# One input projection's start rearranged: w_in stored in order of use on 256-byte rows, x's first tile and the first weights on two queues, and four of k's eight contraction tiles as f16 halves

## What is computed

```python
def first_block(x, pre_mix_norm, w_in, ...):
    xn = _rms_norm(h, pre_mix_norm[l])          # over the 1024 features of a token
    proj = (xn @ w_in[l]).astype(jnp.float32)   # 1024 x 3336
    p_ssd, p_rwkv = jnp.split(proj, [SSD_COLS], axis=-1)
    y_ssd = _ssd_mixer(p_ssd, ...)
    y_rwkv = _rwkv7_mixer(p_rwkv, ...)
    ...
```

## Time and profile before

| | us |
|---|---|
| median of 3 executions | 740.94 |
| lowest, highest | 739.91, 741.89 |
| the profiled execution | 741.43 |
| its span, first to last instruction | 739.6 |
| PE busy in the span | 730.2 (99%) |
| DVE, ACT, POOL busy | 563.0, 434.7, 47.2 |
| bytes moved | 129.43 MB, mean 175 GB/s |

### The profile page before, as it was taken

One profiled execution on the slowest core, in us unless ns is written; L12 is line 12 of the kernel. 1 busy time (PEld: TensorE's weight loads), 2 busy tenths in 40 slices (PEclk: granted clock), 3 DMA queues, 4 the chain that ended last, 5 costly groups with the idle time before them and its releaser, 6 DMA issues.

```text
span 739.6 us, 16490 instructions
## 1 busy us (share of the span) xinstructions
PE 730.2 (99%) x7072; PEld 597.5 (81%) x7072; DVE 563.0 (76%) x893; ACT 434.7 (59%) x690; POOL 47.2 (6%) x81
## 2 busy tenths in 40 slices
PE   9999999999999999999999999999999999999997
PEld 7888877889778888888877696898888888865553
DVE  5699976777879999997668797889685666762453
ACT  5599872523667676666556573387483755653342
POOL 0000133040020000000002000003003000000000
PEclk9999999999999999999999999999999999999999
DMA  9990303512575566546680743339326254566001
GB/s 318 398 400 5 113 18 140 206 38 81 178 278 184 180 207 228 214 173 242 239 331 5 284 168 115 115 116 341 114 102 241 86 213 171 215 228 226 31 0 58
DMA packets 67146, 129.43 MB, mean 175 GB/s; under 512 B 3969, under 2 KB 28033, under 8 KB 66817
## 3 DMA queue, kind: packets, MB, share of 16 engines
q1 hardware_dynamic: 66032, 126.07, 47.3%
q0 software_dynamic: 320, 1.61, 0.6%
q10 hardware_dynamic: 720, 0.70, 0.3%
HBM read 127.32 MB, written 1.05 MB: 174 GB/s over the span
## 4 chain that ended last, share of the span: by engine, by line
PE 83%; DVE 8%; ACT 4%; DMA 2%; SPq 2%; issue 1%; ACTq 0%; DVEq 0%
PE bank L623 38%; PE bank L746 13%; PE bank L3207 11%; PE bank L2533 3%; PE bank L1571 3%; DMA ring<-in_w_in_dram 2%; PE bank L1552 2%; DVE arena L569 2%; SPq L494 1%; PE bank L1834 1%; PE bank L900 1%; PE bank L1887 1%; DVE arena L1082 1%; PE bank L2014 1%; DVE arena L611 1%
## 5 line engine op out<-in xcount | busy, mean ns | idle before, releaser
L623 PE MATMUL bank<-hg,arena 128*128 128x256 f16 x2496 | 275.0, 273 | 0.2 <-DVE hg L648 0.2
L623 PEld LDWEIGHTS bank<-hg,arena 128*128 128x128 f16 x2496 | 243.8, 98 | 30.7 <-issue 1.1
L569 DVE SCALAR_TENSOR_TENSOR arena<-ring,arena 128x1024 f16<-128x1024 f32 x150 | 175.6, 1226 | 58.4 <-ACT arena L537 58.4
L537 ACT ACTIVATE arena<-ring 128x1024 f16<-128x1024 f32 x150 | 146.6, 1044 | 87.6 <-PE bank L3207 37.6
L3207 PE MATMUL bank<-arena 128*128 128x512 f16 (+1 forms) x480 | 83.6, 336 | 0.0
L3207 PEld LDWEIGHTS bank<-arena 128*128 128x128 f16 x480 | 47.0, 98 | 36.1
L746 PE MATMUL bank<-arena 128*128 128x256 f16 x528 | 57.8, 273 | 0.0
L746 PEld LDWEIGHTS bank<-arena 128*128 128x128 f16 x528 | 51.7, 98 | 6.0
L556 DVE SCALAR_TENSOR_TENSOR arena<-ring,arena 128x2048 f16<-128x2048 f32 x22 | 50.4, 2292 | 0.7
L746 PE MATMUL bank<-mix,arena 128*128 128x256 f16 x384 | 42.2, 273 | 0.0
L549 ACT ACTIVATE arena<-ring 128x2048 f16<-128x2048 f32 x22 | 41.7, 1894 | 0.0
(11 more groups left out here) (420 smaller groups left out, 978.0 us busy)
## 6 DMA issues: line engine op xcount, KB each, us to landing
ring<-in_w_in_dram SPq DMA_DIRECT2D x12, 2048.0 KB, 9.0
ring<-in_ffn_w_up_dram SPq DMA_DIRECT2D x22, 1024.0 KB, 7.4
ring<-in_w_ff_dram SPq DMA_DIRECT2D x8, 2048.0 KB, 9.2
ring<-in_w_ff_dram SPq DMA_DIRECT2D x16, 1024.0 KB, 6.5
ring<-in_ffn_w_down_dram SPq DMA_DIRECT2D x11, 1024.0 KB, 6.3
ring<-in_w_out_dram SPq DMA_DIRECT2D x8, 1024.0 KB, 7.3
ring<-in_w_xk_dram SPq DMA_DIRECT2D x2, 2048.0 KB, 10.7
ring<-in_w_xv_dram SPq DMA_DIRECT2D x2, 2048.0 KB, 10.2
```

What stands on the lines that cost most here:

```text
L537: nc.scalar.activation(quarter(halves_of(chunk)[0], chunk, q), quarter(slot(*chunk), chunk, q), ACT.Copy, scale=W_SCALE).then_inc(*mark("w ...
L569: nc.vector.scalar_tensor_tensor(quarter(halves_of(chunk)[1], chunk, q), quarter(slot(*chunk), chunk, q), W_SCALE, quarter(halves_of(chunk ...
L623: mm = nc.tensor.matmul(out_, weight[a][:, k, cols], src[:, k, b, :], start=(first and i == 0), stop=(last and i == 2), skip_group_check=True)
```

## The change

It has four parts.

1. w_in is stored a second time, behind the other data in `parameters`, chunk by chunk in order of use: each partition's row holds a chunk's 8 tiles one after the other (16 KB of a chunk in one piece, 8448 bytes for lora). A row of `parameters` is now 128768 bytes, 503 times 256, and x and each chunk start on a multiple of 256 bytes. lora is one DMA instead of three.
2. The 8 gains stand in front of x and come with its first tile. SP loads gains and x tile 0, k's tile 1, k's 2-3, x 4-7, k's 4-5, 6-7; ACT loads k's tile 0, x 1-3, then all parameters.
3. K_SPLIT goes from 6 to 4: k's contraction tiles 4 to 7 are f16 halves, made in two pieces of two tiles each by ACT and DVE.
4. To make room, the squares of x tiles 4-7 go behind these pieces on ACT, the sums of squares go from DVE to POOL, the gained f32 copy of x tiles 4-7 goes behind lora's low halves on DVE, and the matmul with ones goes between lora's two tiles on PE.

```diff
...
+    def chunk(kind):
+
+        at = W_IN_COLS
+        parts = [(at["w_lo"], 64), (at["a_lo"], 192), (at["dt"], SSD_HEADS)] if kind == "lora" else [(at[kind], 512)]
+        block = np.concatenate([a["w_in"][0][:, c:c + n] for c, n in parts], axis=1)
+        return block.reshape(KT, P, -1).transpose(1, 0, 2).reshape(P, -1)
...
-            load_x(sp, 0, 0, 2)
...
-            first_weights(0, 0, 1)
-            first_weights(1, 1, 1)
-            first_weights(2, 2, 2)
+            load_x(sp, 0, 0, 1)
+            first_weights(sp, 1, 1, 1)
+            first_weights(sp, 2, 2, 2)
             load_x(sp, 2, 4, 4)
-            first_weights(3, 4, 2)
-            first_weights(4, 6, 2)
+            first_weights(sp, 3, 4, 2)
+            first_weights(sp, 4, 6, 2)
...
-        K_SPLIT = 6
...
+        K_SPLIT = 4
...
+        def k_high(act, i):
+            act.wait_ge(*at("first weights", 3 + i))
+            nc.scalar.activation(k16[:, 0, 2 * i:2 * i + 2], slot("w_in", "k")[:, K_SPLIT + 2 * i:K_SPLIT + 2 * i + 2, :],
+                                 ACT.Copy, scale=W_SCALE).then_inc(*mark("k_weights_high", "k high", i))
...
-                if k == KT - 2:
-                    pe.wait_ge(*at("ones landed"))
-                    norm_total(pe, "pre_mix", 4, None)
...
+                if kind == "lora" and j == 0:
+                    pe.wait_ge(*at("ones landed"))
+                    norm_total(pe, "pre_mix", 4, None)
                 if kind == "lora" and j == 1:
-
+                    pe.wait_ge(*at("pre_mix", "gained", KT - 1))
...
         def dve_project1_rwkv(dve):
             lora_low(dve)
+            dve_pre_gain(dve, 1)
             dve.wait_ge(*at("pre_mix", "rstd"))
...
             pool_pads(pool)
+            pool_norm_sum(pool, "pre_mix")
             pool.wait_ge(*at("chunk", CHUNK_NO[("w_in", "r", 0)]))
...
-            act.dma_start(params[:, 0:KT], w["parameters"][:, 0:KT]).then_inc(*mark("gains_landed", "gains landed", by=16))
-            load_x(act, 1, 2, 2)
-            act.dma_start(params[:, KT:], w["parameters"][:, KT:PARAM_COLS]).then_inc(
+            first_weights(act, 0, 0, 1)
+            load_x(act, 1, 1, 3)
+            act.dma_start(params[:, :], w["parameters"][:, 0:PARAM_COLS]).then_inc(
                 *mark("parameters_landed", "parameters landed", by=16))
...
-            for half in range(2):
-                act_pre_norm(act, half)
-                act_pre_high(act, half)
-            k_high(act)
+            act_pre_norm(act, 0)
+            act_pre_high(act, 0)
+            act_pre_high(act, 1)
+            for i in range(2):
+                k_high(act, i)
+            act_pre_norm(act, 1)
             lora_high(act)
             norm_rate(act, "pre_mix", 4)
...
-            for half in range(2):
-                dve_pre_gain(dve, half)
-                for b in (2 * half, 2 * half + 1):
-                    norm_part(dve, nc.vector, "pre_mix", b)
-                dve_pre_low(dve, half)
-            k_low(dve)
+            dve_pre_gain(dve, 0)
+            dve_pre_low(dve, 0)
+            dve_pre_low(dve, 1)
+            for i in range(2):
+                k_low(dve, i)
...
```

More of the change, by code:

```diff
@@ L75 @@
 PARAM_COLS = _n
-X_AT, MEM_AT, FINAL_AT = PARAM_COLS, PARAM_COLS + KT * T, PARAM_COLS + 2 * KT * T
+GAIN_AT = 376
+X_AT = GAIN_AT + KT
+MEM_AT, FINAL_AT = X_AT + KT * T, X_AT + 2 * KT * T
+W_IN_AT = {"k": FINAL_AT + D}
+for _before, _name in (("k", "lora"), ("lora", "r"), ("r", "v"), ("v", "xs"), ("xs", "bc"), ("bc", "z")):
+    W_IN_AT[_name] = W_IN_AT[_before] + KT * (264 if _before == "lora" else 512)
 LEVELS = (2, 4, 8, 16)
@@ L267, in chunk_pieces @@
                 (256, cols[:, :, D_FF + 256 * i:D_FF + 256 * i + 256])]
[L268 to L273, removed]
+    n = KT * (264 if kind == "lora" else 512)
+    return [(0, w["parameters"][:, W_IN_AT[kind]:W_IN_AT[kind] + n].rearrange("p (k n) -> p k n", k=KT))]
 class Ledger:
@@ L451, in load_x, with first_weights @@
         def load_x(queue, i, m, n):
[L453 to L454 removed]
+            a, b = KT + T * m if m else 0, KT + T * (m + n)
+            queue.dma_start(gains_and_h[:, a:b], w["parameters"][:, GAIN_AT + a:GAIN_AT + b]).then_inc(
                 *mark(f"x_landed_{i}", "x landed", i, by=16))
         def x_piece(m):
[L458 removed]
+            return 0 if m == 0 else 1 if m < 4 else 2
+        def first_weights(queue, i, a, n):
+            ((_, k_weights),) = chunk_pieces(w, STREAM[0])
+            queue.dma_start(slot("w_in", "k")[:, a:a + n, :], k_weights[:, a:a + n, :]).then_inc(
+                *(mark(f"first_weights_landed_{i}", "first weights", i, by=16) if i < 4 else
+                  mark("weights_landed_0", "first weights", i, by=16)))
         @block.sync
         def _(sp):
[L462 to L472 removed]
+            load_x(sp, 0, 0, 1)
+            first_weights(sp, 1, 1, 1)
+            first_weights(sp, 2, 2, 2)
             load_x(sp, 2, 4, 4)
[L474 to L475 removed]
+            first_weights(sp, 3, 4, 2)
+            first_weights(sp, 4, 6, 2)
             same(("chunk", 0), ("first weights", 4))
@@ L855, in k_high @@
[L855 to L863, removed]
+                dve.wait_ge(*at("x landed", x_piece(m)))
@@ L865, in pe_project1_first, with k_low @@
+        def k_low(dve, i):
+            dve.wait_ge(*at("k high", i))
+            nc.vector.scalar_tensor_tensor(k16[:, 1, 2 * i:2 * i + 2],
+                                           slot("w_in", "k")[:, K_SPLIT + 2 * i:K_SPLIT + 2 * i + 2, :], W_SCALE,
+                                           k16[:, 0, 2 * i:2 * i + 2], ALU.mult, ALU.subtract).then_inc(
+                *mark("k_weights_low", "k low", i))
         def pe_project1_first(pe):
             for k in range(KT):
-                if k < 2 or k % 2 == 0:
-                    pe.wait_ge(*at("first weights", k if k < 2 else k // 2 + 1))
@@ L870, in pe_project1_first @@
-                pe.wait_ge(*at("pre_mix", "gained", k))
-                if k == K_SPLIT:
-                    pe.wait_ge(*at("k low"))
+                if k < K_SPLIT:
+                    pe.wait_ge(*at("first weights", min(k, 2)))
+                    pe.wait_ge(*at("pre_mix", "gained", k))
+                elif k % 2 == 0:
+                    pe.wait_ge(*at("k low", (k - K_SPLIT) // 2))
                     pe.wait_ge(*at("pre_mix", "low", KT - 1))
@@ L1023, in act_pre_high @@
             for m in range(4 * half, 4 * half + 4):
-                nc.scalar.activation(pre16[:, m, 0, :], h[:, m, :], ACT.Copy, scale=par("pre_mix_norm", m)).then_inc(
+                act.wait_ge(*at("x landed", x_piece(m)))
+                nc.scalar.activation(pre16[:, m, 0, :], h[:, m, :], ACT.Copy, scale=pre_gain[:, m:m + 1]).then_inc(
                     *mark("pre_high", "pre_mix", "high", m))
```

23 lines of the change are left out of this document (10 added, 13 removed).

## The result

The change makes the kernel slower: 745.90 us median of 4 executions (745.44 to 746.54) against 740.59 of 4 before (739.91 to 741.89), ratio 1.0070 with a 95% interval of 1.0054 to 1.0087. That is 5.3 us more, where 740.7 within 739.0 to 742.0 was forecast. The profiled execution took 745.44, with a span of 743.6.

The account below looks back on a forecast made before the run. PE, busy for 41.72 of 42 us between 25 and 67 us, was taken as the bound. r's start gave -0.04 us and the vanished ACT wait +0.33, together 0.3 faster: 740.7 us median, range 739.0 to 742.0.

Parts of the forecast that it names:

- x's second half: Load of x's tiles 4-7 at the start: lands at 8.8 us, where ACT took it up at 9.23 before.
- The log: ACT's log behind the moved matmul with ones: at 21.6 us instead of 18.22.
- The 0.33 ahead of L1673: PE's short wait for ACT at 67.05 us goes, because v lands about 1.6 us earlier: 0.33 us gained.
- POOL's additions: Seven additions of 727 ns on POOL run from 13 to 18 us, before the matmul with ones at 20.8.
- alignment: Starting w_in's pieces on 256 bytes: taken as worth nothing, from 406 GB/s unaligned against 404 aligned.
- k's tile 4: First f16 tile of k on PE: starts at 12.84 us, after PE idles 1.09 us for its halves.
- what r's start gains, 67.05 gains, plus at most 0.33: PE from r's start to 67.05 us: dense, so any gain at r carries through, plus at most 0.33 us.
- Longer pieces may be worth a little: w_in's DMA stream: 420 GB/s seen with rows of 4 and 8 KB, 3.4% more; left to the rivals.
- That v paces: Rival: v's landing sets the pace up to 67.05 us, so its 1.6 us count: 739.3 us, 15%.
- The halves: Rival: k's f16 halves are ready in time, so PE doesn't wait: 1.6 us faster, 739.3 us, 8%.
- The slower one: Rival: x's second half lands at 9.8, the wait for k's low half outweighs the gain: 0.7 us slower, 741.7, 18%.
- slower by over 2.2 us: Whole kernel: a loss beyond 2.2 us needs x later than 11 us or an unseen pace of 16 KB pieces; chance 0.05.

Follow-up runs that it names:

- experiment 10: The changed kernel with 36 further matmuls of unused result on PE ahead of its wait for the table of constants: 745.19 us, ratio 1.0052.
- experiment 1: The changed kernel with padding between the tiles of r, v, xs, bc and z, so these are read in aligned 2 KB pieces: 740.75 us, ratio 0.9998.
- experiment 5: The changed kernel with the table of constants issued by SP behind r's chunk in SP's queue, no longer by POOL: 740.90 us, ratio 0.9993.
- experiment 6: The changed kernel with r, v, xs, bc and z read in pieces of 8 KB: 741.24 us, ratio 1.0010.

## Why the prediction was wrong

**Right, by its own steps.** x's second half: 8.8 forecast, 2.12 + 6.5 = 8.62. lora, for which this holds only with the luck of the next paragraph: 18.24, measured 18.35. The log: 21.6, measured 21.72. r: 25.10, measured 25.23. The 0.33 ahead of L1673: gone. POOL's additions hid, alignment was worth nothing (409 against 410), and the start without the layout came out at a ratio of 0.9994.

**Right by luck in this profile: k's tile 4**, forecast at 12.84 behind an idle time of 1.09, measured at 13.01 without one. PE itself ended its f32 part only at 12.98, because it ran it slowly. The warming matmuls were 0.43 apart to the last, where the last two were 0.22 apart before, and the f32 products behind them kept the slow pace until 7.1. Here are the same 1.8 us in the change and in experiment 10, which has the same start:

```profile
5.20:7.00 1.80, 1.80 (x6) 1.44 (x5) 0.88 (x3) 1.24 (x4) 0.43 (x1) 1.00 1.03 412
```

```profile
5.20:7.00 1.80, 1.80 (x10) 1.49 (x9) 1.15 (x3) 1.34 (x5) 0.65 (x1) 1.00 1.04 414
```

The column of the granted clock says 1.00 in both, but the trace's first record of it stands at 7.20 in the change, at 4.37 before and at 3.91 in experiment 10; the doubled spacing ahead of it is the lower level. So this moment differs between executions of one and the same start, and what decides it is open. Where it came early, the wait was there as forecast, and r came at 24.79:

```profile
12.77 5.41 PE L884 MATMUL bank<-xv,mix 128*128 128x256 f16 x48 [0.99 <-DVE mix L867]
```

**Off by a little.** v was taken up at 27.33, not 30.3, and without a wait: lora as one DMA lifted 11 to 16 us from 306 to 448 GB/s, more than the 406 that I had counted with, and the long pieces took the engines' time from POOL's table. The whole stream gained little: over 16 to 26 us it carried 397 GB/s against 406 before, over 16 to 36 us 401 against 398. v's early landing bought nothing, as PE doesn't wait for v.

**The step that failed** is "what r's start gains, 67.05 gains, plus at most 0.33", together with "Longer pieces may be worth a little". r's start lost 0.17 us and L1664's place 5.3. The first drew, from PE being busy for 41.72 of 42 us, that nothing between 25 and 67 us could make PE wait, without reading how much room each transfer due there had. The table of constants had 1.28 us, and it came 4.0 us too late for PE. The second asked what longer pieces do to the stream that has them, and never what they do to the queue beside it. What the prediction says of the time behind 67 us held: the difference there stayed. The prediction named POOL's additions and SP's and ACT's transfers, and left out POOL's three DMAs, though the words on the kernel before list them. The missing term is 37.22 - 33.02 = 4.2 us by which the dt product came late, and 1.6 us of half clock (0.2 in that product, 1.4 in the 168 behind it), less the 0.5 gained by L1673: 5.3 us.

**The rivals.** That v paces fell. The change itself can't tell, since its wait lies between, but in experiment 1 ACT took up v at 28.52, 3.4 us earlier than before, and L1664's place came at 67.82, 0.8 us later, following r (26.33, 1.3 later). The halves were not in time: PE waited 1.0 us for them in the profiles of experiments 1 and 10, and 0.7 us or less in those in which its own f32 part ended later. The slower one had the right sign with another mechanism (x's second half); it did happen in the profile of experiment 1, where the wait was 1.0 us and the median still 740.75. That "slower by over 2.2 us" needs "a pace of the new 16 KB pieces that no row here shows" was said, at 0.05; but it was their share, not their pace, and the row that would have raised the chance, 9.0 us for 1056 KB on POOL's queue beside a product 1.28 us later, could have been read in the trace of before.

## What to carry to other kernels

Before the pieces of a DMA stream are made longer, list every transfer of another queue that is in flight with it, and read its landing against the start of the instruction that needs it: a slack of 1 us has no row in the waits. The engines serve the queues by turns, and here each KB of piece length made the neighbour's 1.3 MB take 0.54 to 0.60 us longer; put a small table with a due time in the stream's own queue, at its place in the order (experiment 5), or keep the pieces at 2 to 4 KB while it is in flight. And when a wait of some us appears on PE, look at the granted clock behind it: here 4.0 us of waiting cost 1.4 more in the 168 products that followed, while behind the 0.5 us of experiment 6 they took 18.52, as before. Then look which engines queue behind its result before you move it.

## What the runs showed of the hardware that I had not expected

- A piece of 16 KB is one packet and keeps its queue's turn to the end: 10.2, 12.0, 13.6 and 17.8 us for the same three POOL transfers beside pieces of 2, 4, 8 and 16 KB. Pieces of 2112 bytes on POOL's queue go two to a packet (368 packets for 240 with 384 pieces more).
- Long pieces moved more in some stretches: 426 GB/s against 409 with 2 KB pieces between 16 and 20 us, 430 against 403 between 30 and 36. Over 16 to 36 us as a whole it was 401 against 397, and 412 with the table in SP's own queue (experiment 5).
- After 4 us without work for PE, the granted clock was 0.50 for some 3.4 us of dense matmuls (37.9 to 41.3).
- PE's full clock began between 3.9 and 7.2 us in profiles of kernels with the same start, which moves the first f32 product between 4.68 and 5.43 and can hide a wait of 1 us behind it.
- The profile of before has a granted clock of 0.79 over 110 to 118 us, some 80 us behind the last edit; of the variants' profiles six have 0.91 over 105 to 125 us, one 0.93 and the other five 1.00. What decides it is open; it is worth some 1 us, which is why the effects of 1 us here rest on ratios of many executions.
